# Gate and up tiles of two feed-forward parts: hi weights meet x hi and x lo in one product of 512 columns

## The reference, cut to what matters

```
def swiglu(x, w_gate, w_up, w_down):
    return (jax.nn.silu(x @ w_gate) * (x @ w_up)) @ w_down

h = h + 0.5 * swiglu(rmsnorm_2(h, ffn1_norm[l]), ffn1_w_gate[l], ffn1_w_up[l], ffn1_w_down[l])
...   # attention, spatial gating, gates, w_out
h = h + 0.5 * swiglu(rmsnorm_2(h, ffn2_norm[l]), ffn2_w_gate[l], ffn2_w_up[l], ffn2_w_down[l])
```

## Time and profile before

| what | value |
|---|---|
| median of 3 runs | 1124.29 us (1124.07 to 1124.53) |
| span of the profiled execution, first to last instruction | 1122.3 us |
| median less that span | 2.0 us |
| mean granted clock of PE | 0.997 |
| busy PE / PEld | 1113.0 / 1064.4 us |
| busy DVE / ACT / POOL | 721.4 / 665.1 / 731.2 us |

### The profile page before, as it was taken

The page is one execution under the profiler, slowest core; times in us unless marked ns, Lnnn a source line. Parts: engine busy times, 40 slices in busy tenths (PEclk is TensorE's granted clock), DMA queues, the critical chain, the costliest instruction groups (busy, mean ns, idle before and its releaser), DMA issues.

```text
span 1122.3 us, 22370 instructions
## 1 busy us (share of the span) xinstructions
PE 1113.0 (99%) x8976; PEld 1064.4 (95%) x8976; DVE 721.4 (64%) x1273; ACT 665.1 (59%) x1098; POOL 731.2 (65%) x575
## 2 busy tenths in 40 slices
PE   9999999999999999999999999999999999999997
PEld 7888999999988899899999999999899999999997
DVE  6886655576589665375848655556769567655554
ACT  7676854575567577356647544446567447544444
POOL 5787697568488869865865555545865674544442
PEclk9999999999999999999999999999999999999998
DMA  9553354556455544545666766664644665766650
GB/s 336 172 194 119 129 180 153 175 157 221 153 174 184 160 132 150 174 150 169 197 206 208 224 193 200 192 189 151 208 150 131 207 193 165 226 188 191 196 178 38
DMA packets 63895, 199.49 MB, mean 178 GB/s; under 512 B 6992, under 2 KB 17968, under 8 KB 63792
## 3 DMA queue, kind: packets, MB, share of 16 engines
q1 hardware_dynamic: 61920, 194.99, 54.5%
q10 hardware_dynamic: 1872, 3.08, 0.8%
HBM read 196.21 MB, written 1.84 MB: 176 GB/s over the span
## 4 chain that ended last, share of the span: by engine, by line
PE 96%; ACT 2%; DMA 1%; DVE 1%; issue 0%; SPq 0%; POOLq 0%; ACTq 0%
PE ps L1734 51%; PE ps L1832 19%; PE ps L1810 14%; PE ps L1992 2%; PE ps L1783 1%; DMA raw<-in_w 1%; PE ps L2169 1%; ACT ring L481 1%; PE ps L2089 1%; PE ps L2066 1%; PE ps L2027 1%; PE ps L1966 0%; PE ps L2053 0%; PE ps L2069 0%; PE ps L2090 0%; PE ps L2236 0%
## 5 line engine op out<-in xcount | busy, mean ns | idle before, releaser
L367 POOL TENSOR_TENSOR ring<-raw,ring 128x512 fp32r<-128x512 f32 x514 | 698.9, 1366 | 365.0 <-ACT ring L481 344.0
L1734 PE MATMUL ps<-xs,ring 128*128 128x256 f32 x5040 | 597.6, 278 | 0.4 <-DVE mq L1049 0.3
L1734 PEld LDWEIGHTS ps<-xs,ring 128*128 128x128 f32 x5040 | 582.9, 188 | 3.6 <-issue 1.3
L481 ACT ACTIVATE ring<-raw 128x1024 fp32r<-128x1024 f32 x364 | 383.7, 1058 | 214.9 <-PE ps L1734 119.1
L1832 PE MATMUL ps<-ys,ring 128*128 128x256 f32 x1920 | 224.4, 276 | 0.0
L1832 PEld LDWEIGHTS ps<-ys,ring 128*128 128x128 f32 x1920 | 220.7, 188 | 0.0
L1011 DVE TENSOR_TENSOR ring<-raw,ring 128x1024 fp32r<-128x1024 f32 x107 | 144.7, 1352 | 69.1 <-ACT ring L481 68.4
L1810 PE MATMUL ps<-ring,xs 128*128 128x512 f32 x672 | 164.9, 397 | 0.0
L1810 PEld LDWEIGHTS ps<-ring,xs 128*128 128x128 f32 x672 | 123.6, 188 | 26.8 <-issue 1.3
L1324 DVE SCALAR_TENSOR_TENSOR ca<-ps,par,ca 128x253 f32<-128x253 f32 (+2 forms) x96 | 46.0, 479 | 34.4 <-ACT ca L564 33.0
L1478 DVE SCALAR_TENSOR_TENSOR ca<-ps,rms 128x256 f32<-128x256 f32 x44 | 18.6, 423 | 48.6 <-PE ps L1734 48.6
(11 more groups left out here) (290 smaller groups left out, 1029.1 us busy)
## 6 DMA issues: line engine op xcount, KB each, us to landing
raw<-in_w SPq DMA_DIRECT2D x364, 512.0 KB, 3.6
y<-bias_rows SPq DMA_DIRECT2D x6, 256.0 KB, 4.4
out_y<-y SPq DMA_DIRECT2D x4, 256.0 KB, 2.3
const<-in_const SPq DMA_DIRECT2D x1, 896.0 KB, 11.7
bias_rows<-lg ACTq DMA_DIRECT2D x1, 768.0 KB, 8.2
x<-in_x ACTq DMA_DIRECT2D x1, 512.0 KB, 4.2
x<-in_x SPq DMA_DIRECT2D x1, 512.0 KB, 6.4
dec<-in_wT ACTq DMA_DIRECT2D x1, 512.0 KB, 3.7
```

What stands on the lines that cost most here:

```text
L367: last = pool.tensor_tensor(ring[:, g % RING, 1, part], raw[:, g % RAW, part], ring[:, g % RING, 0, part].bitcast(F32), ALU.subtract)
L481: act.activation(ring[:, g % RING, 0, :], raw[:, g % RAW, :], ACT.Copy).then_inc(S["hi"], 1)
L1734: last = mm(ps[bank][:, half * T:(half + 1) * T], ring[:, slot % RING, wp, (at + k) * P:(at + k + 1) * P], rhs(k, xp), start=(first and i ...
```

## The change

For tiles 2 to 21 of both FFNs, gate and up: hi weights by x hi and hi weights by x lo become one matmul of 512 columns that fills the whole bank (x hi's result in columns 0 to 255, x lo's in 256 to 511). Lo weights by x hi stays a matmul of 256 columns into the lower half. ACT copies the upper half to a tile in SBUF (`gq` or `gk`, which the FFNs didn't use), DVE adds the lower half to it, and goes on from the sum. Tiles 0 and 1, and the down slots, are as before. The diff shows ACT (`low_half`, `tile`), DVE (`both_halves`, `gate`, `up`) and PE (`wide_product` and its calls).

```diff
+                def low_half(f, which, slot):
+                    act.wait_ge(S["slots_used"], slot + 1)
+                    act.activation((gq, gk)[which][:, f % 2, :], ps[2 * (f % 2) + which][:, T:2 * T], ACT.Copy)\
+                        .then_inc(S["ffn_low"], 1)
                 def tile(f):
                     p = at + 4 + 3 * (f - 2)
+                    low_half(f, 0, p)
                     next_split(p)
                     gate_tanh(f)
+                    low_half(f, 1, p + 1)
                     next_split(p + 1)
                     product_hi(f)
...
+                def both_halves(f, which, slot):
+                    if f < 2:
+                        dve.wait_ge(S["slots_used"], slot + 1)
+                        return ps[2 * (f % 2) + which][:, 0:T]
+                    dve.wait_ge(S["ffn_low"], (40 if last else 0) + 2 * (f - 2) + which + 1)
+                    low = (gq, gk)[which][:, f % 2, :]
+                    step(tt(low, ps[2 * (f % 2) + which][:, 0:T], low, ALU.add))
+                    return low
                 def gate(f, slot):
-                    dve.wait_ge(S["slots_used"], slot + 1)
-                    stt(ex[:, 2 + f % 2, :], ps[2 * (f % 2)][:, 0:T], -0.5, rms[:, 0:T], ALU.mult, ALU.mult)\
+                    stt(ex[:, 2 + f % 2, :], both_halves(f, 0, slot), -0.5, rms[:, 0:T], ALU.mult, ALU.mult)\
                         .then_inc(S["ffn_t"], 1)
                 def up(f, slot):
-                    dve.wait_ge(S["slots_used"], slot + 1)
-                    stt(ca[:, f % 2, :], ps[2 * (f % 2) + 1][:, 0:T], -0.5, rms[:, 0:T], ALU.mult, ALU.mult)\
+                    stt(ca[:, f % 2, :], both_halves(f, 1, slot), -0.5, rms[:, 0:T], ALU.mult, ALU.mult)\
                         .then_inc(S["ffn_u"], 1)
...
+            def wide_product(bank, slot):
+                for k in range(KT):
+                    mm(ps[bank][:, :], ring[:, slot % RING, 0, k * P:(k + 1) * P],
+                       xs[:, k, :, :].rearrange("p a t -> p (a t)"), start=(k == 0), stop=False, skip_group_check=True)
+                    last = mm(ps[bank][:, 0:T], ring[:, slot % RING, 1, k * P:(k + 1) * P], xs[:, k, 0, :],
+                              start=False, stop=(k == KT - 1), skip_group_check=True)
+                return last
...
-                    tile_product(2 * (f % 2), 0, slot, xs_part).then_inc(S["slots_used"], 1)
+                    wide_product(2 * (f % 2), slot).then_inc(S["slots_used"], 1)
                     here(slot + 1)
                     if f == 2:
                         pe.wait_ge(S["ffn_u"], h_done + 1)
-                    tile_product(2 * (f % 2) + 1, 0, slot + 1, xs_part).then_inc(S["slots_used"], 1)
+                    wide_product(2 * (f % 2) + 1, slot + 1).then_inc(S["slots_used"], 1)
```

More of the change, by code:

```diff
@@ L271, in build @@
         dve_steps act_steps pool_steps slots_used evac gated
-        sq ssq var0 rms0 end_out end_x end_sq end_fold end_var end_rms end_r end_ps end_xg end_sb u_hi u_lo early xs_free sq_sum last_f ffn_t ffn_u x_lo gatef gateln arow gateT gateT_ev iwT iwT_ev rows dec_d dec_e dec_m emr_in
+        sq ssq var0 rms0 end_out end_x end_sq end_fold end_var end_rms end_r end_ps end_xg end_sb u_hi u_lo early xs_free sq_sum last_f ffn_t ffn_u ffn_low x_lo gatef gateln arow gateT gateT_ev iwT iwT_ev rows dec_d dec_e dec_m emr_in
         gl_ps gl_x gl_abs gl_ln gl_cum lev_d lev_e lev_q lev_k lev_ps lev_ev levx_ev
```

## The result

| | before | changed |
|---|---|---|
| median | 1124.18 us | 1137.81 us |
| ratio | | 1.0121 (1.0108 to 1.0135) |
| span of the profiled execution | 1122.3 us | 1136.5 us |
| busy DVE / ACT / POOL | 721.4 / 665.1 / 731.2 us | 774.2 / 685.3 / 732.0 us |

A forecast was written before the change was run, and what follows sets the result against it. PE, busy throughout the FFN stretch, was taken as the bound. Terms 1.5 + 0.5 = +2.0 us on a span of 1122.3 gave 1124.3, and an expected median of 1126.2 us (+0.17%), range 1123.3 to 1129.4.

The forecast's parts named there:

- the first term: Gate and up on PE: 640 times one matmul of 512 at 229.0 ns replaces two of 256 (226.7 ns), +1.5 us.
- my upper end: Wide matmuls of gate and up at the slowest pace seen for 512 columns, 233.3 ns each: 4.3 us lost.
- the down slots keep 2.72 us: Unchanged down slots of the FFNs: stay at 2.72 us; a change of their time would show the prediction wrong.
- Rival 2: Gate and up on PE: wide matmuls fall into the slow 233.3 ns pace, +4.8 us, 1129.1 us; chance 0.22.
- rival 1: Gate and up on PE: the 6.7 ns above the stream belong to each matmul, -3.8 us, 1120.5 us; chance 0.13.
- The rule of the Trainium skill: Matmuls on PE: a fixed 2.5 ns for each matmul whatever its width; by that alone 1.6 us would be saved.
- ACT's copies, DVE's adds, later splits at no price: Two copies and two adds a tile, splits 0.4 us later: hidden by slack inside the FFNs, price 0.
- Behind the first FFN: End of the first FFN: two down slots of 2.72 us stand ahead of the wait for tile 21, price 0.
- The new wait of up for gate by way of ACT: DVE's up waits for its gate through ACT's tanh and second copy; costs nothing in the steady state.
- The end of the second FFN: Wait for tile 21: chain 0.89 us longer against 0.43 us slack, PE waits 0.46 us, +0.5 us (0 to 0.9).

The follow-up runs named there:

- the second experiment: All copies and adds of the change, but three matmuls of 256 columns as in the kernel before: 1125.13 us, ratio 1.0010 (1.0000 to 1.0019).

## Why the prediction was wrong

The step that failed is the first term, "PE: two matmuls of 256 become one of 512", +1.5 us. Its cost was taken as a property of one matmul, read where wide ones stand among wide ones, and multiplied by 640. What decides is the rhythm that a mixture puts the engine into: 235 + 118 ns a pair instead of 229 + 113.3, a term of +8.5 us (40 tiles at 5.65 us instead of 5.44). The wide one came out a little above my upper end (235 ns against 233.3), but even there I had left its narrow neighbour at 113.3.

The second failure is of scope: "the down slots keep 2.72 us" stood there as a condition, without a price, and their change of time was named as a sign of being wrong. They took 2.83; with the 60 matmuls of the next stage that is 4.7 us in all. Rival 2 named the slow pace and its sign, but for the changed matmuls only.

The trace of before had the evidence. I read the pace of narrow matmuls only in the FFNs, where it is always 113.3; in the mixer of the second block the same line has both paces, side by side. This is the kernel before, the chain:

```profile
821.47 0.22 PE ps L2256 x2
821.69 2.74 PE ps L1734 x24
...
824.98 0.43 PE ps L2236 x2
825.41 2.83 PE ps L1734 x24
```

Same instructions, 3% apart for the slot. No matmul of 512 columns runs between the fast slot and the slow one. The slow slot follows one plain float32 matmul of 256 columns (L2236, two records), the fast one follows one of 128 (L2256), and so it goes on in the trace for three more such pairs. A plain float32 matmul is therefore found ahead of either pace. That it sets the pace isn't shown: DVE differs too, busy for 2.76 us beside the slow slot and for 0.14 beside the fast one. A term of mine for "narrow matmuls enter the second pace" would have been (2.83 - 2.72) us x 42 down slots = 4.6 us, and the same 4.4 ns on each narrow neighbour, 640 x 4.4 = 2.8 us.

Point by point:
- Sign of the first term: right, and rival 1 (a fixed part saved by each matmul) is refuted in every kernel with wide matmuls. The rule of the Trainium skill that stood beside it ("TensorE: Matmul & The Clock Gate", Back-to-back issue gap, N/2.4 + 2.5 ns) is not what these runs show: 512 columns took 225 to 236 ns and 256 took 113.3 or 117.8. That section of the Trainium skill gives the formula for a matmul by itself, which my citation left out, and about 131 ns at 512 columns for a stream of weight loads and matmuls; these runs are far from that as well.
- ACT's copies, DVE's adds, later splits at no price: right inside the FFNs. In the run with narrow matmuls and all copies and adds the FFNs keep 5.44 and 2.72 us, and the add takes 0.424 us, not stretched by POOL. Behind the first FFN, which the prediction put at nothing, that run loses about 0.3 us.
- The new wait of up for gate by way of ACT, at no price: right by the same run.
- The end of the second FFN, +0.5 us (0 to 0.9): right in place, too small in size. PE's timeline in the changed kernel, to be read against the two of the second experiment:

```profile
1116.68 2.99 PE L2194 MATMUL ps<-ys,ring 128*128 128x256 f32 x24
1120.15 5.89 PE L2194 MATMUL ps<-ys,ring 128*128 128x256 f32 x48 [0.49 <-DVE ys L1081]
1125.88 0.33 PE L2371 MATMUL ps<-const,y 128*128 128x1 f32 x2
```

From 1116.68 to 1125.88 are 9.20 us, against 8.19 in the kernel before. 0.1 us of that is the slow pace of the first 24, so the end costs 0.9 us. At 117.8 ns the 24 would have let the next one start at 1119.51; it starts at 1120.15, 0.64 us late, and the matmuls behind the wait take some 0.3 us more than at 113.3 ns. The prediction compared the end of DVE's work with a time of the chain, which for running matmuls lies some 0.16 us behind their start, and had no term for the first matmuls behind a wait.

The whole price of copies and adds, by the ratio of the run with narrow matmuls, is 1.1 us with an interval of 0 to 2.1 us. The 0.86 us at the last tile and 0.3 us behind the first FFN make up about that. In the changed kernel, where PE is slower, no wait of PE is recorded behind the first FFN.

What stays open is what the rhythm is inside the engine. Shown are two stable paces, a single wide matmul or three that lead from the fast one to the slow one, and two in a row or one plain float32 matmul of 128 columns that lead back. Whether some plain float32 matmuls leave a stream slow, as those of L2236 may in the kernel before, is open too. What is out of step isn't visible in the trace: a weight load is recorded 3 to 4 ns behind the start of a matmul in the fast pace, 2 to 5 in the slow one. Five in a row, and a wide width between 256 and 512, weren't tried.

## What to carry to other kernels

On an engine that is busy throughout, price a changed instruction by its pace in a stream of the same mixture, and if the trace has none, time that mixture by itself. Look for the same line at two paces anywhere in the trace before taking one of them as its cost, and put a price on the unchanged neighbours too. Merging two float32r matmuls of 256 columns into one of 512 saved no time in any order tried here.

## What the runs showed of the hardware that I had not expected

- TensorE streams float32r matmuls of 256 columns at 113.3 or at 117.8 ns each, at the same granted clock of 1.00, and stayed at either for some 175 us in an FFN and the stage behind it.
- One matmul of 512 columns in such a stream took it from the first to the second (+6.4 us here), three did too, two did not, and two brought a slow stream back; so did one plain float32 matmul of 128 columns. In the kernel before, four slots right behind one plain float32 matmul of 256 columns ran at 117.8 ns.
- In turn with narrow ones, 512 columns take 235 ns; in pairs in a fast stream 226 and 236; eight in a row alternate between 231 and 236 behind a first of 226.
